# A fused attention and feed-forward kernel: corrected durations in the planner that writes every engine's order

## The reference, cut to what matters

```
h = rms_norm(x);  glu_in, q, k, v, gate_logits = split(h @ w_in)
a = a_val * sigmoid(a_gate)
a = causal_depthwise_conv(a, conv_w, conv_b)        # 31 taps for each of 1024 channels
y_a = silu(rms_norm(a)) @ w_conv_out
q, k = rms_norm over each head of 64                 # sums of squares of each row of a head
y_b = softmax-mixed dilated window attention(q, k, v) @ w_attn_out
x = x + (g_a * y_a + g_b * y_b) @ w_out
x = x + (silu(conv3(h2 @ w_up)_gate) * conv3(...)_val) @ w_down
```

## Time and profile before

| what | value |
|---|---|
| time, median of 3 | 1671.2 us |
| the profiled execution, its own time | 1672.42 us |
| its span, first to last instruction | 1670.6 us |
| PE busy | 1548.7 us (93%) |
| DVE busy | 1293.7 us (77%) |
| POOL busy | 931.9 us (56%) |
| ACT busy | 773.8 us (46%) |
| mean granted clock of PE | 0.972 |

### The profile page before, as it was taken

One profiled execution on the slowest core, in us unless ns is written; L12 is line 12 of the kernel. 1 busy time (PEld: TensorE's weight loads), 2 busy tenths in 40 slices (PEclk: granted clock), 3 DMA queues, 4 the chain that ended last, 5 costly groups with the idle time before them and its releaser, 6 DMA issues. The chain is left out here.

```text
span 1670.6 us, 22085 instructions
## 1 busy us (share of the span) xinstructions
PE 1548.7 (93%) x7740; PEld 1311.2 (78%) x7740; DVE 1293.7 (77%) x2088; ACT 773.8 (46%) x1381; POOL 931.9 (56%) x773
## 2 busy tenths in 40 slices
PE   7988778999999999999999999989999899999986
PEld 6766668988878888888888878877877788887866
DVE  5999999999865568817826669978787838889987
ACT  4111246656643334414424344367755326676642
POOL 3656356556736546545545563566757337767562
PEclk9999989999999999999999999999999999999998
DMA  5212122232232223322322242323333212222111
GB/s 187 74 65 88 51 89 86 73 101 89 70 126 91 99 88 101 101 92 98 101 94 90 95 138 68 120 70 102 100 89 110 70 51 77 63 64 68 59 38 51
DMA packets 49069, 145.74 MB, mean 87 GB/s; under 512 B 6784, under 2 KB 9344, under 8 KB 48960
## 3 DMA queue, kind: packets, MB, share of 16 engines
q1 hardware_dynamic: 48960, 144.34, 26.8%
HBM read 130.55 MB, written 2.10 MB: 79 GB/s over the span
## 5 line engine op out<-in xcount | busy, mean ns | idle before, releaser
L367 POOL TENSOR_TENSOR w_lo<-w_raw,w_hi 128x512 fp32r<-128x512 f32 (+1 forms) x442 | 645.9, 1482 | 401.0 <-ACT w_hi L346 387.5
L336 PE MATMUL bank<-x_hi,w_hi 128*128 128x512 f32 x872 | 351.7, 403 | 12.4 <-ACT w_hi L346 6.4
L346 ACT ACTIVATE w_hi<-w_raw 128x1024 fp32r<-128x1024 f32 (+2 forms) x206 | 212.8, 1040 | 315.7 <-PE bank L336 311.3
L336 PE MATMUL bank<-x_hi,w_lo 128*128 128x512 f32 x872 | 345.7, 396 | 9.8 <-POOL w_lo L367 9.6
L336 PE MATMUL bank<-x_lo,w_hi 128*128 128x512 f32 x872 | 344.7, 395 | 0.0
L336 PEld LDWEIGHTS bank<-x_hi,w_lo 128*128 128x128 f32 x872 | 166.4, 191 | 47.8 <-POOL w_lo L367 11.4
L336 PEld LDWEIGHTS bank<-x_hi,w_hi 128*128 128x128 f32 x872 | 166.9, 191 | 46.0 <-ACT w_hi L346 7.1
L336 PEld LDWEIGHTS bank<-x_lo,w_hi 128*128 128x128 f32 x872 | 167.3, 192 | 31.0
L336 PE MATMUL bank<-w_lo,x_hi 128*128 128x256 f32 (+1 forms) x448 | 151.3, 338 | 14.8 <-POOL w_lo L367 14.8
L336 PE MATMUL bank<-a_hi,w_hi 128*128 128x512 f32 x416 | 162.0, 389 | 0.0
L336 PE MATMUL bank<-a_hi,w_lo 128*128 128x512 f32 x416 | 161.8, 389 | 0.0
(11 more groups left out here) (214 smaller groups left out, 3274.8 us busy)
## 6 DMA issues: line engine op xcount, KB each, us to landing
w_raw<-in_weights SPq DMA_DIRECT2D x223, 512.0 KB, 3.6
k_both<-k_both SPq DMA_DIRECT2D x48, 128.0 KB, 2.3
turned<-raw SPq DMA_DIRECT2D x74, 64.0 KB, 2.0
alibi<-in_alibi SPq DMA_DIRECT2D x16, 256.0 KB, 2.8
w_raw<-in_weights SPq DMA_DIRECT2D x8, 384.0 KB, 3.0
r<-in_x SPq DMA_DIRECT2D x8, 256.0 KB, 6.3
r<-in_x SPq DMA_DIRECT2D x4, 512.0 KB, 6.2
out_y<-r SPq DMA_DIRECT2D x16, 128.0 KB, 1.8
```

The source lines that it names most:

```text
L336: return e.matmul(out, lhsT, rhs, start=start, stop=stop, skip_group_check=resumed)
L346: return self.act.run(lambda e: e.activation(out, in_, func, **kw), after, 0.07 + size(out) * 0.00086 + 0.09 * len(kw))
L367: return self.pool.run(lambda e: e.tensor_tensor(out, a, b, op), after, 0.06 + size(out) * 0.00225)
```

## The change

It has three parts.

1. **Duration of a matmul in the plan.** Before, columns / 2400 us (0.213 for 512 columns, at least 0.053); now 0.0105 + 0.000425 per column (0.228 for 512), at least 0.06. A full fp32 one is 0.112.
2. **DVE and POOL meet.** A new method `meet` is called for every POOL `tensor_tensor` and `tensor_scalar`, and for DVE's `tensor_tensor` and `scalar_tensor_tensor` when neither input is in PSUM (`banked`). It keeps one time, `shared`, until which such an operation holds what the two engines share. When the next one would begin before it (by up to 2 us), the difference is added to its duration. POOL's own durations change a little (`tensor_tensor` of 512: 1.21 to 1.25; `tensor_scalar` of 512: 0.67 to 0.66).
3. **Squares of query and key rows.** Before, the copy and the square in `head_rows` waited for the token that `square_free` held when the generator was started; now `head_rows` first waits, in the plan, until the reduction of the square numbered one less is on DVE's queue, and takes that token alone.

No arithmetic is added or removed. Counted over the whole order, DVE has 2022 instructions for 2042, POOL 790 for 777, ACT 1262 for 1255, PE 7686 as before and SP 418 as before.

```
+    def meet(self, engine, after, cost):
+
+        begin = max(engine.time, through(after))
+        if begin < self.shared < begin + 2.0:
+            cost += self.shared - begin
+        self.shared = begin + cost
+        return cost
...
     def mm(self, out, lhsT, rhs, start, stop, after=(), signal=False, resumed=False):
-        cost = max(out.shape[-1], P) / 2400 * (1 if lhsT.dtype == F32R else 4)
+        cost = max(0.06, size(out) * 0.000425 + 0.0105) if lhsT.dtype == F32R else 0.112
...
     def v_stt(self, out, a, s, b, op0, op1, after=()):
-        return self.dve.run(lambda e: e.scalar_tensor_tensor(out, a, s, b, op0, op1), after, 0.07 + size(out) * 0.00115)
+        cost = 0.07 + size(out) * 0.00115
+        if not (banked(a) or banked(b)):
+            cost = self.meet(self.dve, after, cost)
+        return self.dve.run(lambda e: e.scalar_tensor_tensor(out, a, s, b, op0, op1), after, cost)
...
     def p_tt(self, out, a, b, op, after=()):
-        return self.pool.run(lambda e: e.tensor_tensor(out, a, b, op), after, 0.06 + size(out) * 0.00225)
+        cost = self.meet(self.pool, after, 0.06 + size(out) * 0.00233)
+        return self.pool.run(lambda e: e.tensor_tensor(out, a, b, op), after, cost)
...
     def p_ts(self, out, a, s1, s2, op0, op1, after=()):
-        return self.pool.run(lambda e: e.tensor_scalar(out, a, s1, s2, op0, op1), after, 0.06 + size(out) * 0.0012)
+        cost = self.meet(self.pool, after, 0.25 + size(out) * 0.0008)
+        return self.pool.run(lambda e: e.tensor_scalar(out, a, s1, s2, op0, op1), after, cost)
...
     def head_rows(self, kind, pp, n, b, tok):
-        free = self.turned_rows[j] + self.square_free
+        m = self.n_squares
+        self.n_squares += 1
+        free = (yield from self.know(self.squares_done, m - 1)) + self.turned_rows[j]
...
-        self.square_free = [t3]
+        self.squares_done[m] = [t3]
```

More of the change, by code:

```diff
@@ L186, in size, with banked @@
     return math.prod(ap.shape[1:])
+def banked(ap):
+    return type(ap.tensor).__name__.startswith("PSum")
 class Bank:
@@ L313, in __init__ @@
         self.act_full = False
+        self.shared = 0.0
         self.dma_time = 0.0
@@ L351, in v_tt @@
     def v_tt(self, out, a, b, op, after=()):
-        return self.dve.run(lambda e: e.tensor_tensor(out, a, b, op), after, 0.07 + size(out) * 0.00106)
+        cost = 0.07 + size(out) * 0.00106
+        if not (banked(a) or banked(b)):
+            cost = self.meet(self.dve, after, cost)
+        return self.dve.run(lambda e: e.tensor_tensor(out, a, b, op), after, cost)
     def v_ts(self, out, a, s1, s2, op0, op1=None, after=()):
@@ L1097, in head_rows @@
         yield [t2]
-        m, y, w = self.pair_m, self.pair_y, self.pair_t
+        mean, y, w = self.pair_m, self.pair_y, self.pair_t
         src = sq.rearrange("p (h d) -> p h d", d=64)
-        t3 = self.dve.run(lambda e: e.tensor_reduce(m[:, 8 * n:8 * n + 8], src, mybir.AxisListType.X, ALU.add), [t2] + self.norm_done,
+        t3 = self.dve.run(lambda e: e.tensor_reduce(mean[:, 8 * n:8 * n + 8], src, mybir.AxisListType.X, ALU.add), [t2] + self.norm_done,
                           0.07 + S * 0.00106)
-        self.square_free = [t3]
+        self.squares_done[m] = [t3]
         if n == 0:
@@ L1107, in head_rows @@
         inv = self.h_inv.rearrange("p (t o) -> p t o", o=1).to_broadcast([P, NT, 4])
-        m3, y3 = m.rearrange("p (t h) -> p t h", t=NT), y.rearrange("p (t h) -> p t h", t=NT)
+        m3, y3 = mean.rearrange("p (t h) -> p t h", t=NT), y.rearrange("p (t h) -> p t h", t=NT)
         tok = self.v_stt(m3, m3, 1.0 / 64, inv2, ALU.mult, ALU.mult, self.first_rows + [t3] + self.wide_ready["h"])
-        tok = self.v_ts(m, m, 1e-6, None, ALU.add, after=[tok])
-        tok = self.rsqrt(m, y, w, tok)
+        tok = self.v_ts(mean, mean, 1e-6, None, ALU.add, after=[tok])
+        tok = self.rsqrt(mean, y, w, tok)
         tok = self.v_tt(y3, y3, inv, ALU.mult, [tok])
@@ L1441, in first_mixers @@
         self.turned_rows = {j: self.glu_done[KT - 2] + self.glu_done[KT - 1] for j in range(2)}
-        self.square_free = []
+        self.n_squares, self.squares_done = 0, {-1: []}
         self.zero_rows(self.k_lo_first, self.glu_done[KT - 1])
```

## The result

The changed kernel takes 1713.05 us (median of 4 runs, 1712.48 to 1714.9) against 1670.21 for the kernel before on the same chips (4 runs, 1668.37 to 1671.32): ratio 1.026, 95% interval 1.0242 to 1.0277. It is slower by 43 us. Its profiled execution took 1714.9 us, with a span of 1713.1 (before 1670.6).

The account below looks back on a forecast made before the run. PE was busy 1548.7 of 1670.6 us, with DVE nearly full wherever PE is idle early. The terms +69 - 4 - 13 + 2 - 3 = +51 on 1671.2 gave 1722 us, range 1697 to 1746.

Parts of the forecast that it names:

- Step 1: Until the last value eviction: fewer taps queued ahead of it bring it from 196.0 to 150 us, 46 us won.
- Step 2: From the last value eviction to the first `pt_lo`: 144 extra taps and more put it at 320 us, 69 later.
- Steps 3 and 4: After the first `pt_lo`: 4 us from work already done, 13 back in the heads, 2 lost at PE's slow restart.
- Step 5: Elsewhere, mainly the stick-breaking mixer: subtractions move from DVE to POOL, copies to ACT; -3 us, bounds -16 to +8.
- B: Same block, but POOL finds work during it and contends with DVE: +26 us, 1748 us; chance 0.10.
- C: Heads bound by DVE, so the 70.6 us of taps gone from them come back whole: 1665 us; chance 0.03.
- turning point of 58 us: PE's gain between the first product and the end of the heads above which C was to decide.
- D: No change: the early 46 us and all idle time elsewhere are won, 1678 us; chance 0.06.
- E: PE not stopped, its queue having other work ahead of the bank; only the early gain stays, 1625 us; chance 0.01.

Follow-up runs that it names:

- experiment 3: Changed kernel, but a `weave` turn that finds nothing to do takes `pop()`, not another tap, once channel tiles 0 to 3 are done; 1683.52 us.
- experiment 2: Kernel before, with all taps that are left queued on DVE behind head 0's first transposes; 1709.6 us against 1671.53.
- experiment 1: Changed kernel with `meet` handing the duration back as it is; new matmul and POOL durations and the squares stay; 1712.78 us against 1671.53.
- experiment 6: Kernel before, with the new matmul duration in the plan only from the stick-breaking mixer on; 1685.41 us against 1670.73.
- the pair 1.6 and 3.0: Changed kernel, `pop()` first, DVE's planned lead over PE 1.6 us until the heads' dense work, then 3.0, 0.5 from the sparse mixer; 1652.98 us.

## Why the prediction was right

Predicted 1722, measured 1713.05 and within 1697 to 1746; the mechanism was the one forecast, a block of taps that stalls PE. By its steps:

- **Step 1** (last value eviction at 150): 145.6, so -50 for -46. The two reached it together, as expected: DVE waited there 2.37 and 0.61 us for PE. The predicted 10 us for the low clock were too many. Only the first matmuls of the changed kernel, from 6.87 to 14.3 us, are 0.42 apart, at the 1.2 GHz level, which costs some 4 us; from there on they are 0.23 apart:

```profile
13.41 0.63 PE L342 MATMUL bank<-x_hi,w_hi 128*128 128x512 f32 x1
13.84 0.62 PE L342 MATMUL bank<-x_lo,w_hi 128*128 128x512 f32 x1
...
14.53 0.40 PE L342 MATMUL bank<-x_hi,w_hi 128*128 128x512 f32 x1
14.76 0.40 PE L342 MATMUL bank<-x_lo,w_hi 128*128 128x512 f32 x1
```

Behind this start the granted clock was 1.00 up to 150 us, where the kernel before had 0.94, and waits of 14.3 us for `w_lo`:

```profile
0.00:150.00 150.00, 124.44 (x498) 98.90 (x498) 132.21 (x160) 42.19 (x58) 74.78 (x50) 0.94 0.30 102
```

```profile
PE bank L336 <- POOL w_lo L367: 14.3, 5, 5.1
```

- **Step 2** (170 us from there to the first `pt_lo`): 173.9. The taps of the block start 0.66 us apart (1.69 or so only beside one of POOL's squares, as at 253.42), and the first `pt_lo` comes to +68.7 for +69. PE's one gap is 91.8 us, but between 215 and 320 it is idle for 103.9 in all, over the 80 to 100 forecast, since a gap of 18.7 us ends at 228; that one, for the sums of squares and the scaled rows that stand between the taps, was in the text as a wait of the transposes, without a price. The cause named (all turns of `weave` take `aside()`, never `pop()`) is what experiment 3 undid: first `pt_lo` at 232.2.
- **Steps 3 and 4** (-4 -13 +2 = -15): between the first and the last product -20.6 (193.4 for 214.0). Work that changed place accounts for 5.1 of it: 8,192 columns more stand ahead of the first product (3.7 us, for 4 predicted), and 3,072 fewer ahead of the last (1.4, not in the prediction). The matmuls after the gap are 0.42 apart at first, half of the rate, from 320.9 to about 324.7: 3.8 us at the 1.2 GHz level, 1.9 us lost for 2, most of it ahead of the first product. The rest, 15.5, is idle time and clock that came back, for 13 assumed and 17 as the bound: PE was busy 191.64 of 193 us at clock 1.00, where the kernel before was busy 202.82 of 214 at 0.98.
- **Step 5** (-3 elsewhere): -4.7 by the plain marks, -6.1 with the work counted out. It is of the size of the 3 forecast, up to twice as much, and its place is another. The stick-breaking products gain 1.9, PE's waits for `pt_lo` and `sp_lo` falling from 11.1 to 7.3; 5.1 came in the projections ahead of them, which the step left out; the other stretches lose 0.9 together.

The marks add up to the difference of the two spans: +68.7 at the first `pt_lo`, -0.9 from there to the first product, -20.6 and -4.7 make +42.5. The prediction had +51; most of the rest is steps 3 and 4, which gave back 6 us more than it took.

The rivals. B, a block with POOL's work in it, did not come: POOL was busy 10.77 of 105 us in the block, and the squares and `w_lo` there are the ones counted in step 2. This row of POOL's timeline shows that it had nothing to do:

```profile
253.40 1.26 POOL L388 TENSOR_TENSOR ext<-ext,pad_hi 128x512 f32<-128x512 f32 x1 [20.96 <-ACT pad_hi L352]
```

C, heads bound by DVE, is refuted by experiment 2 (13.4 us back, 51.2 lost). Its turning point of 58 us doesn't follow from the prediction's own terms; 69 - 4 + 2 - 3 = 64 is what it would have had to give back. D counted on all the idle time after 990 us, 43 us; some 7 of it came. E is refuted by the gap.

What the prediction left out stands beside a right number. It took the matmul's duration for a small matter ("alone it would allow DVE 7% more taps per matmul"). The 7% were right: 149 taps stand ahead of the last `r1v` in experiment 1 for 138. Small they were not: in the order without the meeting the new duration costs 41 us together with POOL's; alone, in one stage, it costs 10 us in the products (experiment 6). That step 5 came out small seems to hold only in the company of the meeting. The third part, the squares, wasn't timed by itself. Put alone into the kernel before, it leaves the order of every engine as it is. Nor does the third experiment's edit change that order, in which tiles 0 to 3 are done before the first head wants them.

Left open: how the loss of experiment 1 (17.6 us up to the end of the heads, 41 in all) divides between the matmul's and POOL's durations, where the 5.1 us in the projections come from, and which property of the order makes the pair 1.6 and 3.0 the best of those tried.

## What to carry to other kernels

When durations of a planner change, read the new order for a series of one side task's work (a fallback that emits without advancing the planned clock makes one), count what stands ahead of the row that another engine waits for, and price it by the spacing that the trace shows for it without contention, and what stands between by rows of its own; that gave +69 for a measured +68.7. Do not take a correction for harmless because it is nearer to the truth: two errors of a plan can cancel, and here each corrected without the other cost 41 and 59 us, both 43, and both with the fallback mended and the slack set anew gained 18, at the best of the slacks tried. Before two orders are compared at a mark, count the work that stands ahead of it in each: 8 of experiment 6's 18.5 us, and nearly all of the 6.4 that it seemed to win ahead of them, were only columns on the other side of the mark. Side work that has a deadline is late or early in many places at once, so look for the next consumer behind the one that was relieved (the gates behind `pt_lo`), and keep a knob to the stage it is meant for.

## What the runs showed of the hardware

PE's granted clock up to 150 us, behind the slow start, was 1.00 in the changed kernel against 0.94 before. PE was busy 141.00 us there for 124.44, but did 58,112 columns more, which are 26.1 us at 0.45 ns each: not only the 14.3 us of short waits for `w_lo` came back, but half-rate work too. This had not been expected.

After 91.8 us of standstill PE was at half rate for 3.8 us only, which lost 1.9 us, the 2 of the prediction. At this one gap it was the length of the standstill that cost, not the restart.
